# An MLP's down phases: an adding DMA makes a quarter of the low weights, and a fourth seven-product step

## The reference

```python
# block 1
h = rms_norm(x, norm_mlp_g[l])
x = x + jnp.square(jax.nn.relu(h @ w_mlp_up[l])) @ w_mlp_down[l]
# block 2
u = rmsnorm(x, g_mlp) @ w_up
return x + jnp.square(jax.nn.relu(u)) @ w_down
```

## Time and profile before

| what | value |
|---|---|
| median of 3 runs | 2650.54 us (2650.3 to 2650.7) |
| the profiled execution, its own time | 2650.98 us |
| its span, first to last instruction | 2649.3 us |
| TensorE busy | 2640.2 us |
| VectorE busy | 1986.9 us |
| ScalarE busy | 1366.9 us |
| GpSimd busy | 30.3 us |
| moved by DMA | 511.06 MB, 193 GB/s in the mean |

### The profile page before, as it was taken

How to read it: one execution, slowest core, us unless ns; L and a number is a source line. 1 busy time by engine, 2 the same in 40 slices (tenths; PEclk the granted TensorE clock), 3 DMA queues, 4 the chain that set the end, 5 groups by cost and what they waited for, 6 DMA issues and landing times.

```text
span 2649.3 us, 39598 instructions
## 1 busy us (share of the span) xinstructions
PE 2640.2 (100%) x13478; PEld 2233.5 (84%) x13478; DVE 1986.9 (75%) x2876; ACT 1366.9 (52%) x1865; POOL 30.3 (1%) x64
## 2 busy tenths in 40 slices
PE   9999999999999999999999999999999999999999
PEld 7888888888888888888888888888788888888887
DVE  6687876555555778798797567878787978879886
ACT  6455555444444554555554454456555555455453
POOL 0100000000000000000000000000000000000000
PEclk9999999999999999999999999999999999999999
DMA  7655556665655566556566555545555655655565
GB/s 277 236 175 182 190 173 197 204 201 194 203 191 188 177 199 205 187 196 198 190 206 210 190 176 175 173 150 191 171 175 190 199 198 192 205 190 196 187 205 175
DMA packets 141721, 511.06 MB, mean 193 GB/s; under 512 B 16134, under 2 KB 16439, under 8 KB 141464
## 3 DMA queue, kind: packets, MB, share of 16 engines
q1 hardware_dynamic: 136312, 493.86, 55.9%
q0 software_dynamic: 3840, 12.86, 1.5%
q10 hardware_dynamic: 1440, 2.62, 0.3%
HBM read 505.08 MB, written 4.21 MB: 192 GB/s over the span
## 4 chain that ended last, share of the span: by engine, by line
PE 96%; DVE 2%; ACT 1%; DMA 0%; issue 0%; SPq 0%; ACTq 0%; DVEq 0%
PE acc L1955 26%; PE acc L1952 13%; PE acc L1973 5%; PE acc L1991 4%; PE acc L1993 4%; PE acc L1992 4%; PE pS L1991 3%; PE pS L1993 3%; PE pT L1993 3%; PE pT L1991 3%; PE pS L1992 3%; PE pT L1992 3%; PE acc L1970 2%; PE pO L1991 2%; PE pO L1993 2%; PE pG L1993 2%
## 5 line engine op out<-in xcount | busy, mean ns | idle before, releaser
L1104 DVE TENSOR_TENSOR wlo<-raw,whi 128x1024 fp32r<-128x1024 f32 x938 | 1143.4, 1223 | 446.4 <-ACT whi L614 440.5
L614 ACT ACTIVATE whi<-raw 128x1024 fp32r<-128x1024 f32 x938 | 990.0, 1057 | 793.7 <-PE pT L1993 243.1
L1955 PE MATMUL acc<-a_w,whi 128*128 128x512 f32 x2944 | 935.8, 397 | 0.1
L1952 PEld LDWEIGHTS acc<-a_w,wlo 128*128 128x128 f32 x2944 | 553.2, 188 | 129.4
L1952 PE MATMUL acc<-a_w,wlo 128*128 128x256 f32 x2944 | 578.6, 278 | 0.0
L1955 PEld LDWEIGHTS acc<-a_w,whi 128*128 128x128 f32 x2944 | 451.5, 189 | 2.5 <-DVE a_w L1157 0.8
L1973 PE MATMUL acc<-a_w,whi 128*128 128x512 f32 x592 | 198.4, 404 | 0.0
L825 ACT ACTIVATE t<-acc 128x256 f32<-128x256 f32 x128 | 48.9, 382 | 170.0 <-PE acc L1955 169.9
L1970 PEld LDWEIGHTS acc<-a_w,wlo 128*128 128x128 f32 x592 | 111.4, 188 | 24.5
L1970 PE MATMUL acc<-a_w,wlo 128*128 128x256 f32 x592 | 116.8, 279 | 0.0
L1500 DVE TENSOR_TENSOR t<-acc,t 128x256 f32<-128x256 f32 x128 | 54.0, 422 | 74.9 <-ACT t L825 74.8
(11 more groups left out here) (496 smaller groups left out, 3962.8 us busy)
## 6 DMA issues: line engine op xcount, KB each, us to landing
raw<-stream SPq DMA_DIRECT2D x938, 512.0 KB, 3.4
gbias<-gateb POOLq DMA_DIRECT2D x12, 256.0 KB, 4.1
X<-x_rows POOLq DMA_DIRECT2D x4, 512.0 KB, 6.8
bias_scratch<-brow POOLq DMA_DIRECT2D x8, 256.0 KB, 5.5
q<-bias_scratch POOLq DMA_DIRECT2D x8, 256.0 KB, 3.8
out<-X ACTq DMA_DIRECT2D x8, 256.0 KB, 5.3
xF<-x SPq DMA_DIRECT2D x6, 256.0 KB, 6.8
bias<-bias_scratch POOLq DMA_DIRECT2D x8, 128.0 KB, 4.1
```

The source lines that it names most:

```text
L614: A(whi[:, slot, :], raw[:, slot, :], ACT.Copy).then_inc(s.hi_done, 1)
L1104: TT(wlo[:, slot, :], raw[:, slot, :], whi[:, slot, :].bitcast(F32), SUB).then_inc(s.lo_done, 1)
L1952: low = lambda: MM(ps[:, 0:T], wl, wide[:, k0 + k, 0:T], start=False, stop=False, skip_group_check=True)
L1955: last = MM(ps, wh, wide[:, k0 + k, :], start=start and k == 0, stop=not start and k == KC - 1, skip_group_check=True)
```

## The change

Three things change.

- **Low weights by DMA.** In the six groups with two halves, the second chunk of each pair that is no step (four pairs in each half, 8 of 32 chunks of a group, 48 in all) gets its low weights in another way. ScalarE writes `-raw`, rounded as high part, to `wlo` and then `whi` as before. GpSimd waits for the first of these and issues a DMA that adds the chunk, read from HBM once more, to `wlo`. VectorE leaves out its subtraction for these chunks and only clears one column of a small tile (`marks`) to keep the count `lo_done`. TensorE waits for the DMA too, in `weights_ready`.
- **A fourth step.** The second half has steps at pairs 1, 3, 4 and 5 instead of 2, 4 and 5.
- **Warm-up.** Eight instead of five matmuls of 384 columns on zeroes run before the first real one.

```diff
-WARM = 5
+WARM = 8
-BLOCK_ORDER = ((4, 0, 5, 1, 6, 2, 7, 3), (3, 4, 0, 5, 1, 2, 6, 7))
-BLOCK_STEPS = ((0, 1, 2, 3), (0, 1, 2))
+BLOCK_ORDER = ((4, 0, 5, 1, 6, 2, 7, 3), (4, 0, 5, 1, 2, 3, 6, 7))
+BLOCK_STEPS = ((0, 1, 2, 3), (0, 1, 2, 3))
+ADD_CHUNKS = {}
+for _l, _g in SECOND_GROUPS:
+    for _q in range(2):
+        for _t in range(8):
+            if BLOCK_ORDER[_q][_t] not in BLOCK_STEPS[_q]:
+                ADD_CHUNKS[(B_MLP2 if _l else B_MLP1) + 64 * _g + 32 + 16 * _q + 2 * _t + 1] = len(ADD_CHUNKS)
+NADD = 4
...
+            def add_weights(low, high):
+                for c, k in ADD_CHUNKS.items():
+                    if low <= c < high:
+                        pool.wait_ge(s.minus_hi, k + 1)
+                        pool.dma_start(wlo[:, c % NSLOT, :], stream[c], accum_op=ALU.add).then_inc(lo_added[k % NADD], 16)
...
+                if not c.terms and c.base in ADD_CHUNKS:
+                    A(wlo[:, slot, :], raw[:, slot, :], ACT.Copy, scale=-1.0).then_inc(s.minus_hi, 1)
                 A(whi[:, slot, :], raw[:, slot, :], ACT.Copy).then_inc(s.hi_done, 1)
...
                 dve.wait_ge(s.hi_done, c.value(1))
+                if not c.terms and c.base in ADD_CHUNKS:
+                    V.memset(marks[:, ADD_CHUNKS[c.base]:ADD_CHUNKS[c.base] + 1], 0.0).then_inc(s.lo_done, 1)
+                    return
...
+            def weights_ready(c):
+                k = None if c.terms else ADD_CHUNKS.get(c.base)
+                pe.wait_ge(s.lo_done, c.value(1))
+                if k is not None:
+                    pe.wait_ge(lo_added[k % NADD], 16 * (k // NADD + 1))
...
             def chunk_tok(c, i, banks, src, k0, first, last, units=None, corner=False):
                 slot = c.mod(NSLOT)
-                pe.wait_ge(s.lo_done, c.value(1))
+                weights_ready(c)
```

More of the change, by code:

```diff
@@ L179, in __init__ @@
         self.mm_done = make("mm_done")
+        self.minus_hi = make("minus_hi")
         self.evacuated = make("evacuated")
@@ L362, in program @@
         tsm = sb("tsm", 48)[0]
+        marks = sb("marks", 48)[0]
         ssq = tsm[:, 0:16].rearrange("p (s h n) -> p s h n", s=2, h=2)
@@ L478, in program @@
         wg_landed = [ctx.enter_context(nc.semaphore(f"wg_landed{k}")) for k in range(2)]
+        lo_added = [ctx.enter_context(nc.semaphore(f"lo_added{k}")) for k in range(NADD)]
         gb_landed = [ctx.enter_context(nc.semaphore(f"gb_landed{k}")) for k in range(2)]
@@ L574, in _ @@
                     pool.dma_start(gbias[n % 2], gateb[:, D * g + COLS * q:D * g + COLS * q + COLS]).then_inc(gb_landed[n % 2], 16)
+            def add_weights(low, high):
[3 more added lines that the diff above has]
+                        pool.dma_start(wlo[:, c % NSLOT, :], stream[c], accum_op=ALU.add).then_inc(lo_added[k % NADD], 16)
+            add_weights(B_MLP1, B_L2)
             pool.wait_ge(s.m_added, 8)
@@ L595, in _ @@
                     .then_inc(cumb_landed[m % 4], 16)
+            add_weights(B_MLP2, CHUNKS)
         @block.scalar
```

## The result

The changed kernel takes 2746.57 us, the median of five runs (2743.24 to 2752.39), against 2650.54 before: a ratio of 1.0363 with a 95% interval of [1.0349, 1.0377]. I had forecast 2678.0 with a range of 2667 to 2716. The sign was right and the size was not: 96 us longer, where I had 27.5.

What follows compares the result with a forecast made beforehand. TensorE was taken as the bound (96% of the chain), VectorE nearly a second one. 2651.0 + 21.2 (stall, net) + 5.7 (additions) + 0.15 (warm-up) = 2678.1; the median of runs is 0.4 lower: 2678, range 2667 to 2716.

Steps and rivals of the forecast that it cites:

- The fourth step's saving: TensorE, six second halves: three matmuls fewer in each, 18 x 0.227 = 4.1 us saved.
- The stall at m_free: Pair 1 of each second half: TensorE waits about 4.55 us for VectorE to free banks; net 21.2 us over six.
- I take 5.75, between 5.1 and 6.4: Time in us from issue to landing of one 512 KB adding DMA; possible range 3.8 to 8.4.
- rival 2: DMA engines become the bound, from 3.9 us of engine time an addition: 41 us more, 2713; chance 0.06.
- The cover: Time from an addition's issue to TensorE's need: 6.0 us at most pairs, 4.8 at pair 6 of the second half.
- a wait of 0.95 at pair 6: Second half's pair 6: TensorE waits 0.95 us for the addition, six times, 5.7 us in all.
- Rival 1: Adding DMAs take over 6.0 us, so four more chunks a group wait: 2703 at 7 us, 2737 at 8.4; chance 0.24.
- my likeliest case: Stall at m_free and additions landing in 4.8 to 6.0 us: 2672 to 2680 us, chance 0.42.
- The warm-up, 0.15 us: Kernel start: three more warm-up matmuls delay the first real one by 0.15 us, bounds 0 and 2.1.
- Rival 4: VectorE frees the banks in time, so no wait forms at m_free: 5.9 us less, 2644.6; chance 0.08.

Runs made afterwards that it cites:

- The plain copies: The changed kernel with its 48 adding DMAs turned into plain copies of the same size: 2696.01 us, ratio 1.0166.
- the half additions: The changed kernel with each DMA adding only 512 of the 1024 columns: 2703.72 us, ratio 1.0205.
- the last variants: Edits of the kernel before, among them four early additions negated behind sums_hi (2655.79 us) and the fourth step at pairs 2, 4, 5, 6 without additions (2662.7).

## Why the prediction was wrong in size, step by step

**The fourth step's saving, 4.1 us.** Not disputed by any run: the account of the distances closes to 0.2 us with it.

**The stall at m_free, 4.55 us a half.** The mechanism and the size were right, the place only half. The sum of the two waits behind VectorE is 1.43 + 2.96 = 4.39 us a half, in all six. I had put all of it at the fourth matmul of pair 1. My walk through VectorE's queue has weight_sums, the low chunk and then "three corners", and I did not ask who waits for the corners: TensorE wants the bank of the second one in pair 0 itself. So part of the shortage shows at the corner, and what was paid there is not owed at m_free. That no wait forms at pairs 4 and 5 was right. VectorE's subtractions beside GpSimd's issues took 1.22 us, as in the earlier trace rows.

**What failed: "I take 5.75, between 5.1 and 6.4".** It measured 7.6 in the median, and the waits for additions came to 45.0 us where I had 5.7. The price was read as a property of the transfer, from a plain copy at 3.8 that two rows gave. But the two did not stand in the same traffic. In the stretch of the 256 KB row and then in that of the 1024 KB row the weights' queue had

```profile
q1 hardware_dynamic: 228, 0.86, 60.0%
...
q1 hardware_dynamic: 190, 0.71, 29.4%
```

so the slope between them mixes size with company, and the first was among the quickest of its kind. The page of before had the median of all twelve:

```profile
gbias<-gateb POOLq DMA_DIRECT2D x12, 256.0 KB, 4.1
```

The engine time was right at about two passes: 3.16 us against 1.59 for a load. The Trainium skill ("Collectives: The Full Stack", "The bandwidth ceiling") states, for the adds of a ReduceScatter, that they need two source reads where a copy has one. The trace agrees in size, 3.1 us for an addition against 1.7 for a copy by the same queue, and the landing of 5.4 in a quiet stretch is close to the 5.1 that went with it. But the additions run beside a stream whose own share is 54.1%, and there the landing was 9.3 where the loads' was 5.7. The median over all 48 was 7.6. I treated the engines' load as a question of throughput only (rival 2, which decides from 3.9 us of engine time, and at 3.16 rightly did not happen) and not as what stretches each single landing. The plain copies (5.7 us in the median, 15.6 us dearer than no DMA) and the half additions show that the cost falls with the engine time, and the kernel without DMAs shows that all of it, 66.1 us, hangs on them.

**The cover, 6.0 and 4.8 us.** Right: 5.87 and 4.83.

**Which chunks wait.** I expected a wait of 0.95 at pair 6 of the second half alone. It is 2.29 in the group shown, and the odd chunks of pairs 2 and 6 of the first half wait for 3.59 and 2.74. Rival 1 had the right mechanism, but "four waits of 1.0" is not how it goes: a wait makes the stream quiet and the next addition quick, so the waits are fewer and longer. Nor does the wait at m_free get shorter, as rival 1 has it: VectorE's waits are the same to the tenth with and without the DMAs.

**What was missing: the clock.** No term of mine, in the forecast or in a rival, contained it. The granted clock was 1.00 in the stretch that I read the earlier trace rows, and I priced each wait by its own length. After waits of about 3 us it fell: its mean was 0.79 over the 8 us around the first one's end, and the 124 slower distances cost 25 us of the 101. I read that from the profile; no run isolates it. Where the waits were taken away the clock came back with them (0.999 to 1.000 in the last variants). Rival 1 at 7.6 us, between its 2703 at 7 and its 2737 at 8.4, would give 2718; with 25 us of clock 2743, against 2746.6 measured. That this comes so close is partly luck, since rival 1's five short waits and its shorter wait at m_free were both wrong and offset each other. What remains: my likeliest case was missed by the landing time, and that alone puts the sum 2 us above the upper end of my range, 2716. The rest of the way is the clock.

**The warm-up, 0.15 us.** It cost nothing that can be measured, [0.999, 1.0008].

**Rival 4, and what the 48 saved subtractions are worth.** They are worth something: the step costs 41.1 us alone and 29.9 with them. But 11 us of relief were bought for 66 of transfers.

## What to carry to other kernels

The price of a transfer beside a steady load stream was set here by its own engine time and the stream's together. Read the share of the DMA engines in that very stretch, and take a landing time from a row that stood beside the same stream, or else let the range reach to twice the quiet landing (here 5.2 to 10.1). Give a new wait of TensorE of some 3 us a term for the slower matmuls behind it (here 25 us beside 77.5 us of gaps). And when an engine's instruction is moved earlier so as to hide a transfer, look at what then stands behind it: the same move was worth 23 us in one place of ScalarE's queue and 49 one instruction later.

## What was not expected of the hardware

- GpSimd's issue of an adding DMA of 512 KB occupied it for 0.86 us; the issue of the same plain copy for 0.53 (medians of 48 each).
- An addition from HBM into SBUF of 512 KB took 3.16 us of 16 engines in one stretch and 3.1 in the mean, a copy of the same size by the same queue 18.2% of 10 us, 1.82, and 1.7 in the mean. The addition landed between 5.2 and 10.1 us after issue in one execution.
- The clock's fall can come after a wait as well as in it. After the wait of 3.44 us TensorE's distances were 0.43 us only from 1166.06 on, 0.8 us after it had gone on at 1165.26. In the trace's record 8 of the 17 falls began before the wait's end and 9 after it. The Trainium skill ("TensorE: Matmul & The Clock Gate", "Part 1: The HAM clock gate") names two states, at 1.2 and at 2.4 GHz. The trace agrees: away from the changes 0.43 and 0.227 us are the two distances that it shows.
